# The end of a hybrid decoder layer: seven of eight feature rows of the result turned to token order between the last down products, squares and scaling in parts, one root for all token tiles

## The reference

```
x = x + merged @ w_out
f, new_ffn = conv_ffn(rms_norm(x, norm2_g), ffn_conv_buf, w_up, ffn_conv_w, ffn_conv_b, w_down)
x = x + f
y_prompt = rms_norm(x_prompt_rows[:, 16:], final_g)
y_sample = rms_norm(x_sample_rows, final_g)

def rms_norm(x, g):      # over the 1024 features of one token
    return x * rsqrt(mean(x * x) + 1e-6) * g

def conv_ffn(xn, buf, w_up, cw, cb, w_down):
    up = xn @ w_up                                    # 5632 columns
    upc, new_buf = causal_dwconv(up, buf, cw, cb)     # width 3, new_buf = last 2 rows
    val, gate = split(upc)
    return (gelu(gate) * val) @ w_down, new_buf
```

## Time and profile before

| What | us |
|---|---|
| median of 3 runs | 1127.36 |
| the profiled execution's own time | 1126.54 |
| its span | 1124.7 |
| PE busy in the span | 1095.1 |
| end of the last down product's matmuls | 1109.92 |
| from there to the end of the span | 14.78 |

### The profile page before, as it was taken

The page is one execution under the profiler, slowest core; times in us unless marked ns, Lnnn a source line. Parts: engine busy times, 40 slices in busy tenths (PEclk is TensorE's granted clock), DMA queues, the critical chain, the costliest instruction groups (busy, mean ns, idle before and its releaser), DMA issues.

```text
span 1124.7 us, 19318 instructions
## 1 busy us (share of the span) xinstructions
PE 1095.1 (97%) x7995; PEld 1069.9 (95%) x7995; DVE 607.1 (54%) x970; ACT 397.7 (35%) x561; POOL 363.8 (32%) x172
## 2 busy tenths in 40 slices
PE   4999999999999999999999999999999999999996
PEld 3999998999989999899899999999999999999996
DVE  4687354864333242243542338999940289999202
ACT  4466778312432424322423343222211122222213
POOL 4333333332313222222223344333333333433420
PEclk9999999999999999999999999999999999999998
DMA  7222222236345262362452233222323223223302
GB/s 187 58 76 75 57 75 73 63 85 148 79 139 168 64 211 66 85 196 85 141 150 71 79 91 93 83 87 76 116 78 89 57 82 88 76 77 102 96 19 89
DMA packets 180002, 107.69 MB, mean 96 GB/s; under 512 B 8465, under 2 KB 176865, under 8 KB 179920
## 3 DMA queue, kind: packets, MB, share of 16 engines
q1 hardware_dynamic: 179598, 106.39, 33.3%
q10 hardware_dynamic: 322, 0.11, 0.0%
HBM read 94.08 MB, written 12.41 MB: 95 GB/s over the span
## 4 chain that ended last, share of the span: by engine, by line
PE 73%; issue 20%; POOL 5%; DVE 1%; ACT 0%; POOLq 0%; DVEq 0%; ACTq 0%
PE ring L1732 27%; PE ring L2060 22%; PE bank L2060 16%; POOL wlo L773 4%; PE bank L1921 1%; PE bank L1908 1%; PE bank L1961 1%; PE bank L1901 1%; PE bank L1891 1%; PE bank L1949 1%; PE ring L1825 1%; DVE y L1216 1%; PE bank L2091 0%; PE bank L1984 0%; PE bank L1757 0%
## 5 line engine op out<-in xcount | busy, mean ns | idle before, releaser
L773 POOL TENSOR_TENSOR wlo<-stage,whi 128x1024 fp32r<-128x1024 f32 x79 | 194.5, 2463 | 447.7 <-ACT whi L814 447.7
L1732 PE MATMUL ring<-xh,whi 128*128 128x296 f32 x1008 | 227.6, 307 | 0.6 <-POOL wlo L773 0.5
L1732 PE MATMUL ring<-xh,wlo 128*128 128x296 f32 x1008 | 219.6, 299 | 0.0
L1732 PE MATMUL ring<-xl,whi 128*128 128x296 f32 x1008 | 219.5, 299 | 0.0
L1732 PEld LDWEIGHTS ring<-xh,whi 128*128 128x128 f32 x1008 | 163.9, 189 | 6.8 <-issue 4.8
L1732 PEld LDWEIGHTS ring<-xl,whi 128*128 128x128 f32 x1008 | 164.5, 189 | 0.0
L1732 PEld LDWEIGHTS ring<-xh,wlo 128*128 128x128 f32 x1008 | 163.5, 188 | 0.0
L801 POOL TENSOR_TENSOR wlo<-stage,whi 128x1024 fp32r<-128x1024 f32 (+1 forms) x40 | 105.8, 2650 | 176.1 <-ACT whi L1129 176.1
L814 ACT ACTIVATE whi<-stage 128x1024 fp32r<-128x1024 f32 x80 | 84.4, 1056 | 101.7 <-PE ring L1732 88.2
L801 POOL TENSOR_TENSOR wlo_third<-stage,whi_third 128x1024 fp32r<-128x1024 f32 (+1 forms) x20 | 51.5, 2574 | 87.1 <-ACT whi_third L1129 87.1
L1129 ACT ACTIVATE whi<-stage 128x1024 fp32r<-128x1024 f32 (+1 forms) x40 | 45.9, 1153 | 94.4 <-PE ring L2060 59.2
(11 more groups left out here) (337 smaller groups left out, 2283.2 us busy)
## 6 DMA issues: line engine op xcount, KB each, us to landing
stage<-in_w_in SPq DMA_DIRECT2D x56, 512.0 KB, 3.8
stage<-in_w_up SPq DMA_DIRECT2D x44, 512.0 KB, 3.8
stage<-in_w_down SPq DMA_DIRECT2D x16, 704.0 KB, 4.5
stage<-in_w_branch_a SPq DMA_DIRECT2D x8, 512.0 KB, 3.6
c_sample<-in_state_mlstm_C SPq DMA_DIRECT2D x16, 256.0 KB, 5.9
out_s_mlstm_C<-c_sample SPq DMA_DIRECT2D x16, 256.0 KB, 2.4
stage<-in_w_branch_b SPq DMA_DIRECT2D x8, 512.0 KB, 4.2
stage<-in_w_out SPq DMA_DIRECT2D x8, 512.0 KB, 3.8
```

Of the source, the lines that this page charges most:

```text
L773: pool.tensor_tensor(wlo[:, slot, 0:n], stage[:, slot, 0:n], whi[:, slot, 0:n].bitcast(F32), ALU.subtract).then_inc(w_lo, 1)
L1732: last = pe.matmul(out(hf), w[:, kk * P:kk * P + P], x[:, kk, HALF * hf:HALF * hf + HALF], start=kk == 0 and m == 0, stop=kk == kn - 1 and ...
```

## The change

Feature rows 0 to 6 of `resid` are now turned between the steps of the last half's down products 2 to 7, as soon as each is complete, through `bank2(1)`; VectorE copies them to y in SBUF (`turned_out`). The pieces of `new_buf` all go through `bank2(0)`, and the two tables CONV_ and TURN_ say which piece and which feature row stands after the third step (MID) or at the end (END) of product m. ScalarE squares the features in three parts (0 to 3, 4 and 5, 6) as they arrive in SBUF, and VectorE multiplies them by the gain there (`gain_part`). After the last product only feature row 7 is turned, copied, squared (three tiles on ScalarE, two on VectorE) and multiplied by the gain; the sums are added; one root and one reciprocal serve all five tiles; then VectorE scales tiles 0, 2 and 4 and ScalarE 1 and 3, each followed by its store. The area of y moves to that of `xh` and `xl`, which no product reads any more then. Some semaphores and four 5-column sums are new; the list `final` is gone.

```diff
@@ -152,6 +152,15 @@
 FFN_SLOTS = 4
 
 
+CONV_MID = {2: (), 3: (1,), 4: (3,), 5: (5,), 6: (), 7: ()}
+CONV_END = {2: (0,), 3: (2,), 4: (4,), 5: (), 6: (), 7: ()}
+TURN_MID = {2: (), 3: (1,), 4: (3,), 5: (4,), 6: (5,), 7: (6,)}
+TURN_END = {2: (0,), 3: (2,), 4: (), 5: (), 6: (), 7: ()}
+
+TURN_PARTS = ((0, 4), (4, 6), (6, 7))
+TURN_AFTER = {0: (), 1: (), 2: (0, 1), 3: (2, 3), 4: (4,), 5: (5,), 6: (6,), 7: ()}
+
+
 def ffn_tile(h, idx):
 
     return T_FFN + B_HALF * h + idx
@@ -352,8 +361,10 @@
                 return whi3[:, :], wlo3[:, :]
             s = (B_FFN + i % 3 - 1) % 2
             return whi[:, s], wlo[:, s]
-        y = sb("y", [P, TT, D], o_h)
-        fsq = sb("fin_sq", [P, D], o_h + 4 * TT * D)
+        y = sb("y", [P, TT, D], o_a)
+        y7 = sb("y_last", [P, TT, P], o_a + 4 * TT * D)
+        fsq = sb("fin_sq", [P, 4 * P], o_a + 4 * TT * D + 4 * TT * P)
+        dsq = sb("fin_sq_dve", [P, P], o_a + 4 * TT * D + 4 * TT * P + 16 * P)
 
         cols = sb("cols", [P, NROW * P], o_p)
         r = o_p + 512 * NROW
...
@@ -719,7 +732,7 @@
 
             yp, ys = o["y_prompt"][0], o["y_sample"].rearrange("b l d -> (b l) d")
             for i in range(TT):
-                sp.wait_ge(tile_evicted, T_FIN + i + 1)
+                sp.wait_ge(y_act if i % 2 else y_dve, i // 2 + 1)
                 if i == 0:
                     sp.dma_start(yp[0:P - META], y[META:P, 0]).then_inc(y_out, 16)
                 elif i < TT - 1:
@@ -1184,27 +1197,38 @@
                     ffn_hi(i0 + 2 * HK + 3)
                     ffn_hi(i0 + 2 * HK + 4)
                     for n in range(FC):
-                        if n < 3:
-                            ffn_hi(i0 + 2 * HK + 5 + n)
+                        if n % 2 == 0:
+                            ffn_hi(i0 + 2 * HK + 5 + n // 2)
 
                         w_ = min(D, 2 * FF - D * n)
                         if n >= 2:
                             act.wait_ge(f_out[n % 2], 32 * (n // 2))
                         act.wait_ge(fc_done, n + 1)
-                        act.activation(fout[:, n % 2, 0:w_], bank2(n % 2)[0:18, 0:w_], ACT.Copy).then_inc(fc_evicted, 1)
-
-            act.activation(misc[:, 205:206], eps, ACT.Sqrt)
-
-            for i in range(TT):
-                n, t = P if i < TT - 1 else LAST, T_FIN + i
-                act.wait_ge(tile_done, t + 1)
-                if i:
-                    st.wait()
-                st(act.activation(fsq[0:n, :], final[i % 4][0:n, :], ACT.Square,
-                                  accum_out=ssf[0:n, i:i + 1]))
-                st.wait()
-                act.activation(rmsf[0:n, i:i + 1], ssf[0:n, i:i + 1], ACT.Sqrt, scale=1.0 / D, bias=eps[0:n]
-                               ).then_inc(fin_rms, 1)
+                        act.activation(fout[:, n % 2, 0:w_], bank2(0)[0:18, 0:w_], ACT.Copy).then_inc(fc_evicted, 1)
+
+            st(act.activation(misc[:, 205:206], eps, ACT.Sqrt))
+
+            def part_squares(k, f0, f1):
+
+                for i in range(TT):
+                    n = P if i < TT - 1 else LAST
+                    act.wait_ge(turn_out, 2 * f1)
+                    if k or i:
+                        act.wait_ge(sq_parts, TT * k + i)
+                    act.activation(fsq[0:n, 0:P * (f1 - f0)], y[0:n, i, P * f0:P * f1], ACT.Square,
+                                   accum_out=part[k][0:n, i:i + 1]).then_inc(sq_parts, 1)
+            for n, (f0, f1) in enumerate(TURN_PARTS):
+                part_squares(n, f0, f1)
+            act.wait_ge(last_out, 1)
+            for i in range(3):
+                act.wait_ge(sq_parts, 3 * TT + i)
+                act.activation(fsq[:, 0:P], y7[:, i], ACT.Square, accum_out=part[3][:, i:i + 1]).then_inc(sq_parts, 1)
+            act.wait_ge(var_fin, 1)
+            act.activation(rmsf, ssf, ACT.Sqrt, scale=1.0 / D, bias=eps).then_inc(fin_rms, 1)
+            act.wait_ge(gain_fin, 1)
+            act.wait_ge(g_parts, 8)
+            for i in (1, 3):
+                act.activation(y[:, i], y[:, i], ACT.Copy, scale=rmsf[:, i:i + 1]).then_inc(y_act, 1)
 
 
         @block.vector
@@ -1701,17 +1725,62 @@
                 product(HK - 1)
                 product_lo(HK - 1)
                 for m in range(8):
+                    if h and m == 7:
+                        gain_part(2, 6, 7)
                     t, r_ = ffn_tile(h, 2 * HK + m), resid[:, m:m + 1, :]
                     dve.wait_ge(tile_done, t + 1)
                     tt(h2o(r_), ffn_out(B_HALF * h + 2 * HK + m)[:, :, 0:HALF], h2o(r_), ALU.add).then_inc(tile_evicted, 1)
-
-            dve.wait_ge(fg_in, 16)
-            for i in range(TT):
-                n, t = P if i < TT - 1 else LAST, T_FIN + i
-                dve.wait_ge(fin_rms, i + 1)
-                st.link(dve.reciprocal(rmsf[0:n, i:i + 1], rmsf[0:n, i:i + 1]))
-                mul_add(y[0:n, i], final[i % 4][0:n, :], rmsf[0:n, i:i + 1], fgb[0:n, :], ALU.mult, ALU.mult
-                        ).then_inc(tile_evicted, 1)
+                    if not h:
+                        continue
+
+                    def turned_out(f):
+
+                        dve.wait_ge(turned, f + 1)
+                        cpy(y[:, 0:4, P * f:P * f + P], grouped(bank2(1)[:, 0:4 * P], P)).then_inc(turn_out, 1)
+                        cpy(y[0:LAST, 4, P * f:P * f + P], bank2(1)[0:LAST, 4 * P:5 * P]).then_inc(turn_out, 1)
+
+                    def gain_part(k, f0, f1):
+
+                        if k == 0:
+                            dve.wait_ge(fg_in, 16)
+                        dve.wait_ge(sq_parts, TT * (k + 1))
+                        w_ = slice(P * f0, P * f1)
+                        tt(y[:, 0:4, w_], y[:, 0:4, w_],
+                           fgb[:, w_].rearrange("p (o c) -> p o c", o=1).to_broadcast([P, 4, P * (f1 - f0)]), ALU.mult
+                           ).then_inc(g_parts, 1)
+                        tt(y[0:LAST, 4, w_], y[0:LAST, 4, w_], fgb[0:LAST, w_], ALU.mult).then_inc(g_parts, 1)
+                    if m == 6:
+                        gain_part(1, 4, 6)
+                        st.link(tt(ssf, part[0], part[1], ALU.add))
+                    if m == 5:
+                        gain_part(0, 0, 4)
+                    for f in TURN_AFTER[m]:
+                        turned_out(f)
+
+            st.link(tt(ssf, ssf, part[2], ALU.add))
+            dve.wait_ge(fin_turned, 1)
+            st(cpy(y7[:, 0:4], grouped(bank2(0)[:, 0:4 * P], P)))
+            cpy(y7[0:LAST, 4], bank2(0)[0:LAST, 4 * P:5 * P]).then_inc(last_out, 1)
+            st.wait()
+            st.link(stt(out=dsq[:, :], in0=y7[:, 3], scalar=1.0, in1=y7[:, 3], op0=ALU.mult, op1=ALU.mult,
+                        accum_out=part[3][:, 3:4]))
+            dve.wait_ge(last_out, 1)
+            st(stt(out=dsq[0:LAST, :], in0=y7[0:LAST, 4], scalar=1.0, in1=y7[0:LAST, 4], op0=ALU.mult, op1=ALU.mult,
+                   accum_out=part[3][0:LAST, 4:5]))
+            w_ = slice(7 * P, 8 * P)
+            tt(y[:, 0:4, w_], y7[:, 0:4], fgb[:, w_].rearrange("p (o c) -> p o c", o=1).to_broadcast([P, 4, P]), ALU.mult
+               ).then_inc(g_parts, 1)
+            tt(y[0:LAST, 4, w_], y7[0:LAST, 4], fgb[0:LAST, w_], ALU.mult).then_inc(g_parts, 1)
+            dve.wait_ge(sq_parts, 3 * TT + 3)
+            st.wait()
+            tt(ssf, ssf, part[3], ALU.add).then_inc(var_fin, 1)
+            dve.wait_ge(fin_rms, 1)
+            dve.reciprocal(rmsf, rmsf).then_inc(gain_fin, 1)
+            dve.wait_ge(gain_fin, 1)
+            dve.wait_ge(g_parts, 8)
+            for i in (0, 2, 4):
+                n = P if i < TT - 1 else LAST
+                ts(y[0:n, i], y[0:n, i], rmsf[0:n, i:i + 1], None, ALU.mult).then_inc(y_dve, 1)
 
 
         @block.tensor
@@ -2077,31 +2146,49 @@
                     ffn_steps(d0 + m, HK, gh, gl, range(HK - 1), None if m else arrived)
                 for m in range(2):
                     ffn_steps(d0 + m, HK, gh, gl, [HK - 1], None if m else arrived).then_inc(tile_done, 1)
+
+                def conv_rows(n):
+
+                    if n:
+                        pe.wait_ge(fc_evicted, n)
+                    else:
+                        pe.wait_ge(tile_evicted, T_FFN + d0 + 1)
+                    for ft in range(8 * n, min(8 * n + 8, UPT)):
+                        last = pe.transpose(bank2(0)[0:18, P * (ft - 8 * n):P * (ft - 8 * n) + P],
+                                            flast[:, ft, :], ident[:, :])
+                    last.then_inc(fc_done, 1)
+
+                def turn(dst, f):
+
+                    for i in range(TT):
+                        n = P if i < TT - 1 else LAST
+                        last = pe.transpose(dst[0:n, P * i:P * i + P], resid[:, f, P * i:P * i + n], ident[:, :])
+                    return last
+
+                def turn_early(f):
+
+                    pe.wait_ge(tile_evicted, T_FFN + d0 + max(f, 1) + 1)
+                    if f:
+                        pe.wait_ge(turn_out, 2 * f)
```

(36 more changed lines are left out.)

7 lines of the change are left out of this document (5 added, 2 removed).

## The result

| | before | changed |
|---|---|---|
| median (us) | 1127.3, 6 runs (1126.06 to 1127.79) | 1131.28, 6 runs (1130.36 to 1132.56) |
| profiled execution, own time / span (us) | 1126.54 / 1124.7 | 1131.11 / 1129.3 |
| E, end of the last product's matmuls, in the profile | 1109.92 | 1115.25 |
| from E to the first y store's issue | 5.58 | 5.49 |
| from that issue to the end of the span | 9.20 | 8.56 |

The ratio of changed to before is 1.0034, 95% interval 1.0024 to 1.0044: slower by 2.7 to 5.0 us. The forecast was 1129.6, the range 1127.2 to 1131.6. The result lies inside the range, near its upper end. The direction is that of the forecast, and so is the price ahead of E; the gain behind E came out at less than half of what was forecast, and the middle value is 1.7 us short.

A forecast was written before the change was run, and what follows sets the result against it. PE, busy 1095.1 of 1124.7 us, was taken as the bound up to E, then nearly a store stream at 390 GB/s. +4.26 ahead of E and -1.7 behind gave +2.6 us: 1129.6, range 1127.2 to 1131.6.

The forecast's parts named there:

- The sum: Ahead of E: 35 early transposes and four f_last transposes at 0.109 us each on PE, +4.26 us.
- rival 2: Ahead of E: the turns cost no time, 4.26 shrinks to 0.4, change -1.2 us, 1125.7; chance 0.08.
- rival 3: Ahead of E: turns cost more, by latency per group or PE waiting on ScalarE's copies; +3.7 to +6 us; chance 0.10.
- the counted margins: Ahead of E: PE's waits met long before; feature rows turned 2.5 us or more after their addition began.
- rival 4: Behind E: gain not had because ScalarE brings its parts late; +1 to +3 us on top; chance 0.05.
- Rival 5: PE clock between products: a fall to 1.2 GHz in one product would add 9 us; chance 0.02.
- VectorE's branch: Behind E, after the copies: two squares with sums and gain on 512 and 128 columns, done at E + 3.9.
- the slow start: Start of the store burst: 0.4 us at 268 instead of 390 GB/s, losing 0.13 us.
- Rival 1: Behind E: stores bound by issue, not rate; not slower, change +0.3 to +2.2 us, 1127.3 to 1129.2; chance 0.15.
- the rival's condition: Store burst behind E: stores bound by issue is decided from 5.7 us for the bytes, 414 GB/s.
- the forecast's middle: Whole kernel: 1129.6 us, between 1129.1 from the profiled execution and 1130.0 from the median of three earlier runs.
- its forecast alone: Whole kernel without rivals: 1128.6 (414 GB/s, profiled base) to 1130.6 us (362 GB/s, median base); chance 0.60.

The follow-up runs named there:

- The two queues: Changed kernel with the stores of tiles 1 and 3 issued by ScalarE instead of SyncE; 1130.97 us, ratio to before 1.0033.

## Why the prediction came out as it did

**Ahead of E: as worked out.** The sum said +4.26 (35 x 0.109 and 4 x 0.109), and product 2 to E grew by 62.63 - 58.37 = 4.26. Each of the seven groups takes the 0.55 that was taken, neither 0.71 nor nothing, and doubling them doubles the price. So rival 2 (turns for nothing) and rival 3 (dearer turns) fall. (Rival 3's upper end, +6, is less than its own terms give: 2.6 and five times 1 are 7.6. Nothing hangs on it.) PE's waits: none between product 2 and E, the counted margins held. ScalarE had its first part's squares done by 1095.14, ahead of the addition of product 5 (1096.18), 8.96 us from the start of product 5 where 8.9 was counted. VectorE did wait for ScalarE once more, 2.45 us in product 7:

```profile
1112.14 0.69 DVE L1748 TENSOR_TENSOR y<-y,final_g_b 128x512 f32<-128x512 f32 x1 [2.45 <-ACT fin_sq L1218]
```

After it and the 80-row piece behind it VectorE idles 2.25 us until the last addition, so ScalarE was late there and it cost nothing, and rival 4 falls. Rival 5, the clock, falls by the 1.00 over the whole stretch from product 2 to E: groups of 5, 9 and 13 transposes between the products left it at 2.4 GHz.

**Behind E up to the first store: as worked out.** Predicted and measured, from E: turn ended 1.58 and 1.63, copies 2.51 and 2.62, ScalarE's squares 3.7 and 3.92, VectorE's branch 3.9 and 3.96, root ended 4.43 and 4.45, reciprocal 4.71 and 4.67, store issued 5.52 and 5.49. They came from the durations of rows, most of them of another form, and the start-to-start distance of the earlier trace rows. The step with the largest error is ScalarE's, 0.43 a square where 0.38 was worked out, and VectorE hid it, by only 0.04 us. The last tile was ready at E + 6.90 (6.8 predicted).

**The term that was mis-sized: from the first issue to the end.** The forecast had 7.6 us (7.62 by its terms): 0.64 in which nothing moves (no row shows it; the kernel before has 0.7 as well), 0.4 at 268 and the rest at 390 GB/s, 0.8 at the end. Measured were 8.56. Term by term, with 390 GB/s as the measure:
- nothing moves for 0.71 in place of 0.64: +0.07;
- the slow start lasts 1.40 us and carries 0.37 MB, which costs 0.46 and not 0.13: +0.33. I had read the 268 GB/s of the earlier trace rows as the rate of one store in flight and let it end with the second issue. Here the second and third were issued before or within it and it stayed at 263, so it is not the number of stores. It is the store of tile 0: in the kernel before with half the stores, single stores of 128 tokens have 373 and 381;
- the middle, 1.62 MB at 400: -0.10;
- the end: 0.37 MB at 233 GB/s at a share of 0.75, which costs 0.64: +0.64. The forecast had the full rate to the last byte. Part of it is the stores of the last tile (291 GB/s at a full share), part is engines that finish one after another (158 GB/s at 0.40). The earlier trace rows could have warned me: the kernel before had its 390 GB/s at a share of 0.98 only from 1117.80 to 1121.20, and I took that rate for bytes outside that window too; from 1121.20 to 1122.40 its trace has 283 at 0.90.

These sum to 0.94, the difference between 8.56 and 7.62. One reading stands behind most of it: the rate was taken to depend on how many stores are in flight, where it depends on which store moves. The last issue, forecast at E + 7.5, came at E + 9.74 for a reason that the forecast had not seen (long issues behind a full queue). The two queues, with the last issue at E + 7.5, show that it cost nothing, so the error of this step did not enter the time.

**Rival 1** (stores bound by issue, not slower) is refuted from both sides: with the last issue at E + 7.5 nothing is gained, and half the bytes bring 2.9 us. (Half the bytes alone would not refute it, since the issues became shorter too.) The middle of the burst ran at 400 to 406 GB/s at a share of 1.01 or 1.02 in three kernels, which is near the 414 of the rival's condition, but the rate of its middle is not the rate of a burst: 2.36 MB in 7.05 us are 335 GB/s. By the Trainium skill, DMA: Bandwidth & Descriptors, section Bandwidth, HBM would hold such a transfer to about 358 GB/s, and the forecast weighed that figure: the 4.05 us at 400 stand above it here too. That the mean of the burst lies near it is no support, since the parts that make the mean low go with single stores and with engines that have finished.

**The sum.** In the profiles: +4.26 ahead of E, -0.73 behind it (14.78 to 14.05, where -1.7 was forecast), +3.53 in all; and +1.08 by which product 2 began later, which the repeat shows to be within the spread. Between the medians it is 3.98 (interval 2.7 to 5.0): 3.53 lies inside, and the other 0.45 is not explained; the repeat of the changed kernel, at 1129.69, was 0.7 below the lowest of its six runs, so single runs can differ by more than that. Of the 1.7 us between forecast and median, 0.9 is the term above, 0.3 that the median before came out at 1127.3 and not 1127.0, which the forecast's middle amounts to, and 0.5 that rest. (The bounds that the prediction gives for its forecast alone, 1128.6 and 1130.6, come out of its own terms as 1128.8 and 1130.4.)

## What to carry to other kernels

Work moved from behind the last product of a full PE to between its products pays its whole PE time (0.11 us a transpose here), so it must take more than that off the tail; count first what the tail becomes bound by once the work is gone. Here 4.3 us of transposes bought 0.7, because what was left is a burst of stores. Such a burst is not its bytes by the best rate in sight: 2.36 MB took 8.45 to 9.89 us from the first issue to the end, by the order of the stores and the queues. The sum 2.7 us + bytes / 407 GB/s was made from this kernel's full and half version and holds for their order alone; read the rate of each store by itself, and the share beside it. Work that moves to an idle engine instead (squares on ScalarE, the root's table) cost nothing ahead of E in the profiles, but in this tail it bought at most 1 us, too little for the times to show.
